# Two split weight tiles placed 64 bytes further along in SBUF in a two-network fp32 kernel

## The reference, cut to what matters

```
def _layer(x, ...):
    x = x + MACARON * _swiglu(_rmsnorm(x, ffn1_norm), ffn1_w_gate, ffn1_w_up, ffn1_w_down)
    h = _rmsnorm(x, mix_norm)
    p = h @ w_in
    ...
    x = x + jnp.concatenate([y_a, y_b, y_c], axis=-1) @ w_out
    x = x + MACARON * _swiglu(_rmsnorm(x, ffn2_norm), ffn2_w_gate, ffn2_w_up, ffn2_w_down)
```

## The kernel before, in words

| tensor | start | remainder by 128 | remainder by 512 |
|---|---|---|---|
| con (holds the identity) | 16512 | 0 | 128 |
| h | 25568 | 96 | 480 |
| xh, xl | 41952, 58336 | 96 | 480 |
| wraw0, wraw1 | 83904, 92096 | 64 | 448 |
| whi0, whi1 | 100288, 108480 | 64 | 448 |
| wlo0, wlo1 | 116672, 124864 | 64 | 448 |
| raw2_w, raw3_w | 142784, 150976 | 64 | 448 |
| ah_w, al_w | 159168, 171456 | 64 | 448 |
| uh_w, ul_w | 183744, 200128 | 64 | 448 |
| uv_x, wsr_x (a plain float32 product of the mixer) | 165312, 177600 | 64 | 448 |

## Time and profile before

### The profile page before, as it was taken

One profiled execution on the slowest core, in us unless ns is written; L12 is line 12 of the kernel. 1 busy time (PEld: TensorE's weight loads), 2 busy tenths in 40 slices (PEclk: granted clock), 3 DMA queues, 4 the chain that ended last, 5 costly groups with the idle time before them and its releaser, 6 DMA issues.

```text
span 3252.4 us, 47396 instructions
## 1 busy us (share of the span) xinstructions
PE 3209.2 (99%) x20092; PEld 2855.6 (88%) x20092; DVE 2032.9 (63%) x2889; ACT 1416.7 (44%) x2128; POOL 836.4 (26%) x377
## 2 busy tenths in 40 slices
PE   9999999999999999999999999999999999999998
PEld 7887899988778999889998889999899998889997
DVE  6577755445857444486676637667667566466756
ACT  4354544443635444354443324444445333244533
POOL 1210033320500333202322430232123223312322
PEclk9999999999999999999999999999999999999999
DMA  5211223321203232313322322332323223222322
GB/s 174 82 40 55 95 98 117 104 97 62 76 27 110 100 115 100 115 65 105 130 78 91 117 91 71 107 127 79 104 98 119 89 91 117 78 91 98 124 85 78
DMA packets 223219, 308.95 MB, mean 95 GB/s; under 512 B 7872, under 2 KB 151248, under 8 KB 222752
## 3 DMA queue, kind: packets, MB, share of 16 engines
q1 hardware_dynamic: 219424, 291.41, 26.9%
q0 software_dynamic: 3584, 14.52, 1.3%
HBM read 303.80 MB, written 2.10 MB: 94 GB/s over the span
## 4 chain that ended last, share of the span: by engine, by line
PE 70%; DVE 19%; ACT 6%; issue 3%; DMA 1%; POOL 0%; DVEq 0%; SPq 0%; ACTq 0%
PE bank L603 21%; PE bank L605 21%; PE bank L604 21%; DVE wlo L2135 5%; ACT whi L1343 4%; DVE wraw L2157 2%; DVE raw_w L2157 2%; DVE ul_w L2345 1%; PE bank L1001 1%; PE bank L623 1%; DVE zt L2340 1%; DMA wraw<-in_e_w_in 1%; DVE t_w L2340 1%; DVE zt L2196 1%; PE bank L1284 1%
## 5 line engine op out<-in xcount | busy, mean ns | idle before, releaser
L3220 POOL TENSOR_TENSOR wlo<-wraw,whi 128x1024 fp32r<-128x1024 f32 (+1 forms) x189 | 492.5, 2609 | 1318.4 <-ACT whi L1343 1318.3
L603 PE MATMUL bank<-xh,whi 128*128 128x256 f32 (+1 forms) x2456 | 718.2, 292 | 12.3 <-DVE xl L2437 7.9
L605 PE MATMUL bank<-xh,wlo 128*128 128x256 f32 (+1 forms) x2456 | 714.0, 291 | 0.0
L1343 ACT ACTIVATE whi<-wraw 128x1024 fp32r<-128x1024 f32 (+2 forms) x399 | 434.9, 1095 | 633.2 <-PE bank L605 485.5
L604 PE MATMUL bank<-xl,whi 128*128 128x256 f32 (+1 forms) x2456 | 709.8, 289 | 0.0
L3220 POOL TENSOR_TENSOR wlo<-raw_w,whi 128x1024 fp32r<-128x1024 f32 x114 | 291.9, 2564 | 844.9 <-ACT whi L1343 844.9
L603 PEld LDWEIGHTS bank<-xh,whi 128*128 128x128 f32 x2456 | 462.3, 188 | 31.8 <-DVE wlo L2135 11.6
L2135 DVE TENSOR_TENSOR wlo<-wraw,whi 128x1024 fp32r<-128x1024 f32 (+1 forms) x210 | 277.7, 1325 | 317.1 <-ACT whi L1343 316.3
L603 PE MATMUL bank<-whi,uh_w 128*128 128x512 f32 x1216 | 474.4, 390 | 0.6 <-DVE ul_w L2766 0.6
L605 PE MATMUL bank<-whi,ul_w 128*128 128x512 f32 x1216 | 473.4, 389 | 0.0
L604 PE MATMUL bank<-wlo,uh_w 128*128 128x512 f32 x1216 | 473.3, 389 | 0.0
(11 more groups left out here) (402 smaller groups left out, 4970.7 us busy)
## 6 DMA issues: line engine op xcount, KB each, us to landing
wraw<-in_w_in SPq DMA_DIRECT2D x26, 1024.0 KB, 5.0
wraw<-in_ffn_w_gate SPq DMA_DIRECT2D x40, 512.0 KB, 4.3
raw_w<-in_ffn_w_gate SPq DMA_DIRECT2D x40, 512.0 KB, 4.8
raw_w<-in_ffn_w_up SPq DMA_DIRECT2D x40, 512.0 KB, 4.2
wraw<-in_ffn_w_up SPq DMA_DIRECT2D x40, 512.0 KB, 4.3
wraw<-in_ffn_w_down SPq DMA_DIRECT2D x20, 1024.0 KB, 5.0
raw_w<-in_ffn_w_down SPq DMA_DIRECT2D x20, 1024.0 KB, 5.0
raw_w<-in_mlp_w SPq DMA_DIRECT2D x19, 1024.0 KB, 5.0
```

What stands on the lines that cost most here:

```text
L603: M.matmul(o, lh, rh, start=start, stop=False, skip_group_check=more)
L605: return M.matmul(o, ll, rh, start=False, stop=stop, skip_group_check=more)
L1343: A.activation(hi, raw, ACT.Copy).then_inc(*k.w_hi.inc(("hi", j)))
L3220: G.tensor_tensor(lo[:, 0:n], raw[:, 0:n], hi[:, 0:n].bitcast(F), ALU.subtract).then_inc(*k.w_lo.inc(("lo", j)))
```

## The change

Two tensors of 16 float32 per partition (64 bytes) are allocated, one ahead of whi0 and one behind wlo1. Nothing reads or writes them, and no instruction is added, removed or moved.

```
     k.raw = [sb(f"wraw{i}", [128, SLOT]) for i in range(NRAW)]
+    sb("hi_edge", [128, 16])
     k.hi = [sb(f"whi{i}", [128, SLOT], R) for i in range(2)]
     k.lo = [sb(f"wlo{i}", [128, SLOT], R) for i in range(2)]
+    sb("lo_edge", [128, 16])
     k.ident = k.con[:, C_ID:C_ID + 128]
```

## The result

The changed kernel takes 3275.9 us (median of four runs, 3274.43 to 3275.97) against 3253.3 us for the kernel before, a ratio of 1.0068 with a 95% interval of 1.0055 to 1.0080. It is slower by 22.6 us. The forecast was 3225.

The account below looks back on a forecast made before the run. PE was taken to bound the kernel, by matmul count times pace. From 3254.1 us, -8.6 (B) and -20.0 (C), all else 0, sum to -28.6 and 3225.5, stated as 3225; range over the cases 3170 to 3276.

Parts of the forecast that it names:

- B: 256-column matmuls streaming ah_w, up projections, 3888: offset 0 to 64, from 120.0 ns to A's pace, -8.6 us.
- A: 256-column matmuls streaming xh, 6720 at 117.8 ns: offset +32 to -32, taken as 0 us.
- D: 512-column matmuls streaming weights with xh stationary, 2352 at 233.3 ns: offset +32 to -32, taken as 0 us.
- E: 512-column matmuls streaming xh with weights stationary, 624 at 233.3 ns: offset +32 to -32, taken as 0 us.
- F: 256-column matmuls streaming weights with xh stationary, 480 at 118.2 ns: offset +32 to -32, taken as 0 us.
- +32 and -32 pace alike: Products on xh: activation start 32 bytes after or before the weight's, modulo 128, gives the same pace; change 0 us.
- C: 512-column matmuls streaming weights, uh_w or ah_w stationary, 3744 at 226.7 ns: offset 0 to 64, -20.0 us.
- the floor: Lowest start-to-start pace, from a float32 product: 216.0 ns at 512 columns, 109.4 at 256; excess over streaming 2.7 ns.
- The slow rival: Any unequal offset behaves like xh's: B takes A's pace, C takes D's, +16.1 us, 3270; chance 0.24.
- a weight at remainder 0 helps by itself: Weight start at a multiple of 128 bytes removes half of all excess above the floor, 97 us: 3157; chance 0.10.
- nothing repeats beyond 64 bytes: Rival that nothing changes: placement effects repeat every 64 bytes or less, so every class keeps its pace; 3253, chance 0.32.

Follow-up runs that it names:

- the run with 128 bytes: Against the kernel before, ah_w, al_w, uh_w and ul_w moved 128 bytes further from the weights, whi and wlo as before: 3267.7 us.
- that with 256: Against the kernel before, ah_w, al_w, uh_w and ul_w moved 256 bytes further away, weights and xh as before: 3252.8 us.
- the first run: Against the kernel before, only the first small tensor added, so weights, uh_w, ul_w, ah_w and al_w move together to remainder 0: 3254.0 us, ratio 1.0001.
- the one with the down projections put back: Changed kernel with uh_w and ul_w 192 bytes further, so their starts equal the weights' by 256 again: 3251.0 us, ratio 0.9994 to the kernel before.
- the run with the streams at a multiple of 512: Against the kernel before, xh, xl, ah_w and al_w start at multiples of 512 bytes; whi, wlo, uh_w, ul_w keep remainder 448: 3252.1 us, ratio 0.9996.

## Why the prediction was wrong

**What bounds the kernel: right in the main.** PE's busy time has 18.4 of the 20.4 us, and the splits and the waits for weights did not take part. PE's idle time, which was not to rise, rose by 2.0 us: its waits for zt grew by 3.6 and others shrank.

**B, right in size, in part by luck.** Forecast -8.6 us by taking A's row, measured -9.2, and the loads went from 192 to 188 ns as named. But at the same distance of 64 ah_w took 115.4 ns with the activations moved alone and 114.7 with ah_w alone: that it landed on A's pace here does not follow from the distance. What does follow it is the load: at 256 columns the loads beside ah_w record 191 to 192 ns in every kernel whose ah_w products all have equal starts and 187 to 189 in every kernel where all are unequal, and those beside xh went from 188 to 192 when xh was made equal (below). The pace goes its own way: ah_w took from 114.7 to 119.1 ns with such short loads.

```profile
L607 PEld LDWEIGHTS bank<-xh,wlo 128*128 128x128 f32 x2448 | 469.6, 192 | 8.7
```

**A, D, E, F, taken as 0.** D, E and F moved by 0.4 us or less. A moved by +7.4, inside its bound of 15.8. That +32 and -32 pace alike holds at 512 columns and only roughly at 256: the mean went from 118.0 to 118.8 ns, within the 1 ns that the prediction allowed.

**C, the step that failed.** The text put C midway between its pace and the floor, -20.0 us, and set aside D's row, which had the right width and said +24.7; measured +23.3. That is 43.3 of the 49.1 us between the sum of -28.6 and the +20.5 of the classes. Two reasons were given. One was that 64 is as far apart as two starts can be; the run with 128 bytes is unequal and that with 256 is equal, so it is not, and the distance does not matter anyway (16 bytes cost as much). The other was that the excess at offset 0 goes with the weight load, in C as in B, and comes from two reads that meet. C's loads were never long: those beside uh_w record 188 ns in the kernel before, like the ones at unequal starts, and 187 in the changed kernel, where the matmuls are slower:

```profile
L604 PEld LDWEIGHTS bank<-wlo,uh_w 128*128 128x128 f32 x1216 | 228.3, 188 | 46.5
```

```profile
L606 PEld LDWEIGHTS bank<-wlo,uh_w 128*128 128x128 f32 x1216 | 227.8, 187 | 54.8
```

At 512 columns equality is the good case, in C and, when xh was made equal, in D too. The trace had said so: C at offset 0 was the fastest 512-column class by 6.6 ns, and I took its excess for a fault. Nor does any run show a class of fp32r matmuls near the floor of 216.0 ns that the middle was taken from: none had a mean below 226.8 at 512 columns or 114.7 at 256. That floor is the distance between the records of a plain float32 product, which leaves two records per call (the mixer issues four, the timeline has eight), so a call costs 432 ns.

**The rivals.** The slow rival, that any unequal offset behaves like xh's, is what happened in this kernel: B at A's pace and C at D's. The experiments bear it out for C, at every distance tried, and not for B, as said above. Its 3270 lacks only A's 7.4 us. Its condition, C's pace up by more than 2.3 ns, was met with 6.3. I gave it 0.24 although it was the only case built from measured rows at the right widths. That a weight at remainder 0 helps by itself is refuted by the first run and the one with the down projections put back, both equal to the kernel before within 0.1%. That nothing repeats beyond 64 bytes is refuted by the change itself. The Trainium skill ("SBUF — State Buffer", Who interferes with whom) gives TensorE two independent read ports and says that it never waits on anyone. The 3253 that the prediction drew from it did not come: padding alone takes matmuls with the same streams and loads from 227.0 to 233.3 ns. 16 bytes, the line length that the same page of the Trainium skill gives under Specifications (TRN2), are enough to do it.

**The range** held the time, at its edge; the chances had the wrong side ahead.

**What stays open.** Why equal starts by 256 bytes help a 512-column stream and hurt a 256-column one, and how one unequal product slows its neighbours, was not settled; both theories of the single matmul failed. The pace of a 256-column stream also depends on something that was not found: ah_w at a distance of 64 took 114.7, 115.4, 118.3 or 118.4 ns on average in four kernels. Three of these, the ones with 114.7, 115.4 and 118.4, have the same remainders by 512 in both operands. And xh went from 118.0 to between 117.3 and 117.5 ns in the runs with ah_w and al_w displaced by 32 or 128 bytes or alone by 64 either way, and with only the low activations displaced, although neither it nor a weight had moved. So at 256 columns the two starts are not the whole of it. An effect of where the other engines read and write SBUF would be a rival for this; no run tests it. At 512 columns there is an exception as well: class E took 230.0 ns, not 233, at a distance of 64 in the run with the streams at a multiple of 512.

## What to carry to other kernels

Where PE streams back to back and every matmul has its own weight load, compare the start addresses of stream and stationary operand by 256 bytes: in this kernel equal starts were worth about 6 ns of 233 for 512-column fp32r matmuls, unequal ones 1 to 6 ns of 120 for 256-column ones, and the tile's own alignment was worth nothing. Padding one tensor moves all that are allocated behind it, so an alignment change has to be costed by the pairs whose distance it changes. And when a trace holds a row for the case that the change creates, at the right width, take that row rather than an idea of why it should be better.

## What the runs showed of the hardware that was not expected

- The pace of an fp32r matmul depends on whether the starts of its two operands are equal by 256 bytes: 226.8 to 227.0 ns against 232.6 to 233.4 for the 512-column products with uh_w, with 16, 32, 64 and 128 bytes all the same.
- At 256 columns, for products that stream xh or ah_w, the sign is the other way: 120.1 to 120.5 ns when equal, 114.7 to 119.1 when not.
- Where all three products of a triple are alike, a weight load of a 256-column product on ah_w or xh records 191 to 192 ns when the starts are equal by 256 bytes and 187 to 189 when not. For the 512-column products on uh_w it does not follow equality: 188 when equal, 187 to 190 when not.
- One unequal product among the three of a triple costs 12 ns (ul_w displaced) to 15 ns (wlo displaced) per triple; two unequal products cost 19, as much as all three.
- 256 bytes of padding per partition that no instruction touches, 64 ahead of ah_w and 192 behind al_w to keep the other distances by 256, made the kernel 12 us faster (3240.5 against 3252.7 us).
